# Hybrid decoder block on one core: key norms as one number per token, row spreads from rounded halves, the last expert batch in another order

## The chip, the cores and the metric

The kernel runs on one core of a Trainium2 chip. The metric is the device time of one execution in microseconds (us); the kernel before takes 690.97 us (median of 3 runs, 690.14 to 691.37). Its engines work side by side and wait for one another on semaphores: PE (TensorE, matrix products and transposes into the PSUM banks), DVE (VectorE), ACT (ScalarE), POOL (GpSimd) and SP, which issues nearly all the DMAs.

## The reference, cut to what matters

```python
u = rms_norm(h, norm1_w)                       # h: 16 meta tokens and 256 tokens, 1024 wide
proj = u @ W_in                                # differential attention q k v, delta rule q k v, gates
# branch A: differential attention, 8 heads, per-head RMSNorm of the output
# branch B: convolution over 4 tokens and SiLU on q, k, v, then
q = l2_normalize(q) * 128 ** -0.5;  k = l2_normalize(k)
gc = cumsum(g)                                 # log decays, g < 0
decay = where(incl, exp(gc[i] - gc[j]), 0)
kb = k * beta
A = where(strict, (kb @ k.T) * decay, 0);  T = inv(A + eye)
u = T @ (v * beta);  w = T @ (kb * exp(gc))
qk = (q @ k.T) * decay
k_dec = k * exp(gc[-1] - gc)
# along the chunks: v_new = u - w @ S;  o = (q * exp(gc)) @ S + qk @ v_new
#                   S = S * exp(gc[-1]) + k_dec.T @ v_new
o = rms_norm(o, norm_w) * silu(gate)
h = h + (sigmoid(gA) * (yA @ Wa) + sigmoid(gB) * (o @ Wb)) @ W_out
# mixture of experts: 32 experts of 256 hidden columns, 2 for each token
for e in range(32):
    y = y + combine[:, e:e+1] * ((silu(x @ w_gate[e]) * (x @ w_up[e])) @ w_down[e])
out = rms_norm(h + y, final_norm_w)[:, 16:]
```

## The kernel before

**Projections.** The columns of W_in, the two branch matrices and W_out are cut into 96 tiles of 128 columns; `KINDS` gives their order (ak av aq dq dk dv gate ga ya gb yd out). SP loads them in pairs into a ring of six slots. Each 32-bit tile is split into a rounded high part, `w_hi` (ACT, `split_high`, L302), and the rest, `w_lo` (DVE, `split_low`, L307), two tiles ahead; PE then takes 24 products per tile, three for each of 8 blocks (L817): high by high, high by low, low by high. Tiles alternate between two PSUM banks. So tile n waits for its two parts and for tile n-2 to be read out: by ACT (`tile_out`, counted by `tile_copied`), or by DVE alone for ya, yd and out (counted by `mixed`).

**The stage of 26 slots.** For m = 0 to 25 PE computes tile dq+m, and around it the attention heads, the convolution (DVE L1809, L1822) and the sums of squares run. The sums of squares of 8 q heads, 8 k heads and 8 attention outputs gather as 24 rows of one bank, one row by head, one column by token. After slot 20 ACT makes rows of reciprocal roots from them (`roots`, L1463 to L1467: a table load, Ln, Exp). A row must reach all 128 partitions to scale a head; `spread` (L941) does it as a 32-bit product with one column of the identity, into a bank that DVE multiplies from (`scale_by`, L1831 to L1837). In slots 22 to 25 come four spreads each: first the keys, then the queries. The eight spreads of attention follow one by one behind the first eight steps of the delta rule.

**The delta rule.** It runs for the meta tokens, chunk 0 and chunk 1 (128 tokens each) as steps s0 to s7, t1, x2, t2, x3, t3, v, o, q; for the meta tokens s0 to s7, w, m. Chunks work in two chains of four heads, a and b. `MIX_ORDER` puts half tiles of the projection between PE's steps; `BEHIND` is the matching list for ACT, DVE and POOL. In `BEHIND` a tile whose second half stood before a step is held and is read out behind that step's first chain. Step q is the norm of a chunk's output: PE sums the squares (L1110), ACT takes Ln and Exp (L1542, L1543), DVE multiplies (L2013), POOL gates (L735). Ln and Exp are in one ACT table, the tanh of the gates in another; a change costs an ACT_TABLE_LOAD.

Per-token columns hold what depends on a token and a head: `nbeta` (minus beta), `nbegc` (minus beta times exp(gc)), `kdec` (exp of the total less gc), `ngc` (minus gc, the bias in the exponent of the decay, L1501).

**Experts.** 8 batches of 4 experts (`batch`, L1200 on). PE gathers tokens (L1207), multiplies by the gate and the up matrices (L1222), turns the routing weights (L1229) and the hidden values (L1233), multiplies by the down matrices in two halves of columns (L1244), and adds the result to the tokens (L1254; L1194 in the last batch). Weights, 1 MB each, go to 12 slots and 9 twins of them; SP issues a load when its slot is free. The last batch's down matrices come in halves of columns (`load_last`, L578). Then the last norm: squares on ACT (L1651), root (L1592, L1593), scaling on DVE (L2193 to L2210), store (L623).

The wait that holds a tile's readout to its place:

```python
if what[0] == "spread": BEHIND.append(what)
else:
    BEHIND.append(what)
    BEHIND += held
    held = []
```

## Time and profile before

| | before |
|---|---|
| median of 3 runs | 690.97 us (690.14 to 691.37) |
| the profiled execution's own time | 685.91 us |
| its span, first to last instruction | 684.1 us |
| PE busy | 614.6 us (90%) |
| DVE, ACT, POOL busy | 338.8, 267.0, 42.8 us |
| moved by DMA | 156.05 MB |

The profile page has a row for each engine that gives its busy share in 40 equal slices of the span (17.1 us each) and one for the clock granted to TensorE, in tenths of full speed. Below it, the views used here are: the chain of waits (the pieces of work that follow one another to the last instruction), the timeline of one engine (each with the idle time before it and what ended it), and a table by stretches of time. Times are from the span's start.

### The profile page before, as it was taken

The numbers are of one execution on the slowest core, as the hardware profiler recorded it, in microseconds if no ns is written. First come the engines' busy times: TensorE is split into PE (matmuls) and PEld (weight loads), VectorE is DVE, ScalarE is ACT, GpSimd is POOL, SyncE is SP. The second block draws the span as 40 slices with busy tenths as digits, with TensorE's granted clock in tenths as the row PEclk, the third lists the DMA queues.
The fourth block names the chain that finished last, engine by engine and source line by source line (L and its number), as shares of the span: only waits on it lengthen the run. The fifth ranks groups of instructions, "written<-read, shape, count | busy, mean of one in ns | idle before, by whom it ended". The sixth has DMA issues, their size and how long they took to land.

```text
span 684.1 us, 14436 instructions
## 1 busy us (share of the span) xinstructions
PE 614.6 (90%) x5923; PEld 510.8 (75%) x5923; DVE 338.8 (50%) x744; ACT 267.0 (39%) x594; POOL 42.8 (6%) x92
## 2 busy tenths in 40 slices
PE   8999999999999998999899799999888856849864
PEld 7999998889988888999799799987444524425341
DVE  5443449999868658465755378624211101101102
ACT  6355458667686444235332946313101000101003
POOL 8300000000000001100310100000000000000000
PEclk9999999999999999999999999999999979788989
DMA  9945453232333331221321158899999999999992
GB/s 291 325 144 185 145 164 96 91 124 80 107 124 124 124 123 64 64 73 52 95 93 63 62 173 273 360 422 421 396 421 419 421 421 422 422 422 422 421 396 81
DMA packets 71297, 156.05 MB, mean 228 GB/s; under 512 B 7234, under 2 KB 56500, under 8 KB 59460
## 3 DMA queue, kind: packets, MB, share of 16 engines
q1 hardware_dynamic: 70048, 155.06, 60.7%
q8 instruction: 45, 0.74, 0.4%
q10 hardware_dynamic: 1188, 0.12, 0.2%
q14 instruction: 16, 0.13, 0.1%
HBM read 154.12 MB, written 1.05 MB: 227 GB/s over the span
## 4 chain that ended last, share of the span: by engine, by line
PE 61%; DVE 15%; DMA 14%; issue 4%; ACT 4%; ACTq 0%; DVEq 0%
PE bank L817 28%; DMA arena<-in_expert_w_down_dram 11%; PE bank L1244 5%; PE bank L1222 5%; PE bank L998 5%; DMA arena<-in_expert_w_gate_dram 4%; DVE w_lo L307 4%; PE bank L802 3%; DVE arena L1809 3%; PE bank L976 2%; PE bank L1207 2%; PE bank L941 2%; PE bank L1254 2%; DVE arena L1848 1%; ACT w_hi L302 1%
## 5 line engine op out<-in xcount | busy, mean ns | idle before, releaser
L817 PE MATMUL bank<-uT_hi,w_hi 128*128 128x272 f32 (+1 forms) x568 | 171.9, 303 | 5.6 <-DVE w_lo L307 3.9
L817 PE MATMUL bank<-uT_hi,w_lo 128*128 128x272 f32 (+1 forms) x568 | 162.5, 286 | 0.0
L817 PE MATMUL bank<-uT_lo,w_hi 128*128 128x272 f32 (+1 forms) x568 | 162.4, 286 | 0.0
L307 DVE TENSOR_TENSOR w_lo<-arena,w_hi 128x1024 fp32r<-128x1024 f32 x88 | 108.7, 1237 | 53.6 <-ACT w_hi L302 53.2
L817 PEld LDWEIGHTS bank<-uT_hi,w_hi 128*128 128x128 f32 x568 | 107.6, 190 | 10.2 <-issue 8.4
L817 PEld LDWEIGHTS bank<-uT_lo,w_hi 128*128 128x128 f32 x568 | 107.9, 190 | 1.4 <-issue 0.5
L817 PEld LDWEIGHTS bank<-uT_hi,w_lo 128*128 128x128 f32 x568 | 107.8, 190 | 0.0
L302 ACT ACTIVATE w_hi<-arena 128x1024 fp32r<-128x1024 f32 x88 | 92.2, 1052 | 0.5 <-DMA arena<-in_w_in_dram 0.4
L1244 PE MATMUL bank<-arena 128*32 128x512 f32 x256 | 39.8, 775 | 28.3 <-DMA arena<-in_expert_w_down_dram 25.9
L1222 PE MATMUL bank<-arena 128*32 128x256 f32 x1024 | 59.0, 390 | 5.3 <-DMA arena<-in_expert_w_gate_dram 5.3
L1222 PEld LDWEIGHTS bank<-arena 128*32 128x32 f32 x1024 | 33.5, 113 | 28.0 <-issue 7.0
L1244 PEld LDWEIGHTS bank<-arena 128*32 128x32 f32 x256 | 10.3, 137 | 51.5 <-issue 49.4
L1809 DVE SCALAR_TENSOR_TENSOR arena<-arena 128x272 f32<-128x272 f32 x72 | 37.8, 525 | 7.5 <-ACT arena L1380 5.7
L1634 ACT ACTIVATE arena<-bank 128x512 f32<-128x512 f32 x8 | 4.8, 598 | 92.0 <-PE bank L1244 92.0
L998 PE MATMUL bank<-arena 64*64 64x64 f32 x1032 | 37.7, 221 | 1.6 <-DVE arena L1948 1.6
L2156 DVE COPY arena<-bank 128x512 f32<-128x512 f32 x8 | 5.5, 691 | 67.5 <-PE bank L1244 67.5
L998 PEld LDWEIGHTS bank<-arena 64*64 64x64 f32 x1032 | 33.4, 135 | 5.9 <-DVE arena L1948 2.1
L2146 DVE COPY arena<-bank 128x256 f32<-128x256 f32 x8 | 3.4, 424 | 61.3 <-PE bank L1229 61.3
L1207 PEld LDWEIGHTS bank<-arena 128*128 128x128 f32 x256 | 29.8, 192 | 3.8 <-issue 3.8
L1207 PE MATMUL bank<-arena 128*128 128x128 f32 x256 | 30.2, 276 | 0.3 <-DVE arena L2118 0.3
L1628 ACT ACTIVATE arena<-bank,arena 128x128 f32<-128x128 f32 x32 | 9.1, 367 | 49.6 <-PE bank L1207 49.6
L1254 PE MATMUL bank<-arena 128*128 128x512 f32 x56 | 25.9, 605 | 0.0
(346 smaller groups left out, 1023.6 us busy)
## 6 DMA issues: line engine op xcount, KB each, us to landing
arena<-in_w_in_dram SPq DMA_DIRECT2D x36, 1024.0 KB, 5.2
arena<-in_expert_w_gate_dram SPq DMA_DIRECT2D x32, 1024.0 KB, 21.2
arena<-in_expert_w_up_dram SPq DMA_DIRECT2D x32, 1024.0 KB, 23.2
arena<-in_expert_w_down_dram SPq DMA_DIRECT2D x28, 1024.0 KB, 20.1
arena<-in_w_branch_attn_dram SPq DMA_DIRECT2D x4, 1024.0 KB, 5.3
arena<-in_w_branch_dn_dram SPq DMA_DIRECT2D x4, 1024.0 KB, 5.1
arena<-in_w_out_dram SPq DMA_DIRECT2D x4, 1024.0 KB, 5.4
arena<-in_expert_w_down_dram SPq DMA_DIRECT2D x8, 512.0 KB, 15.6
```

Source lines behind the costliest of these rows:

```text
L302: nc.scalar.activation(w_hi[q % NSPLIT], split_source(nc.scalar, q), ACT.Copy).then_inc(w_hi_ready, 1)
L307: nc.vector.tensor_tensor(w_lo[q % NSPLIT], src, w_hi[q % NSPLIT].bitcast(F32), ALU.subtract).then_inc(w_lo_ready, 1)
L802: last = pe.matmul(ps[:, 0:SEQ], a[:, c, t * P:(t + 1) * P], b[i][:, c, :], start=(c == 0 and k == 0), stop=(c == NC - 1 and k == 2))
L817: last = pe.matmul(ps[:, 0:b.shape[2]], a[:, c, :], b[:, c, :], start=(c == 0 and i == 0), stop=(c == NC - 1 and i == 2))
L941: pe.matmul(spread_bank(k)[:, 0:L], ident[:, SPREAD[k]:SPREAD[k] + 1].broadcast_to([P, P]), rs_rows, start=True, stop=True).then_inc(sprea ...
L976: last = pe.matmul(o[:, h, :], lhsT(h), rhs(h), start=start, stop=stop)
L998: last = pe.matmul(o[rows, h, :], lhsT[rows, h, :], rhs[rows, h, :], start=True, stop=True, tile_position=(q * Q, q * Q))
L1207: last = pe.matmul(bank[6 + group][:, (c % 4) * P:(c % 4 + 1) * P], u2[:, t, c * P:(c + 1) * P], pick[:, t].rearrange("p e s -> p (e s)"), ...
L1222: last = pe.matmul(bank[4 + 2 * m][CAP * e:CAP * (e + 1), 0:D_EXPERT], xg[:, c, CAP * e:CAP * (e + 1)], gate_up(e, odd)[:, c, m], start=(c ...
L1244: last = pe.matmul(bank[6 + half][CAP * e:CAP * (e + 1), :], hidT[:, fc, CAP * e:CAP * (e + 1)], down_of(e, odd)[:, fc, half * 512:(half + ...
L1254: last = pe.matmul(bank[2 * t + half][:, :], pickT[:, t, :], dsb[:, half * 512:(half + 1) * 512], start=False, stop=False, skip_group_chec ...
L1809: last = stt(a, x_[:, k:k + L], tap(k, c), a, ALU.mult, ALU.add)
```

## The change

- **Keys.** The keys are no longer scaled by their norms: the 8 key spreads and their 16 DVE products are gone. With r the reciprocal root of a token and head, k appears in A as r_i r_j, once on each side. PE turns the finished rows (three transposes, to bank 7), DVE copies r and the logarithm of its square's inverse out as columns (`key_columns`, slot 23), PE spreads the meta tokens' 16 rows (slot 24), and DVE folds them into the columns above (`fold_keys`, slot 25): `nbk` = nbeta times r, `nbegc` and `kdec` times r, and `ngc` minus half the logarithm, which puts r_j into the decay. `dkT_meta`, formerly written by the scaling, is now a copy on POOL.
- **Spreads.** The rows are made three times, 32 partitions apart (`one_of` has three ones). ACT rounds them to `rs_halves` and DVE takes the rest of the rows 32 to 63 as the low half; a spread is then one rounded product (`two_of` picks row i and row 32+i). 16 are left: 3, 3 and 2 of the queries' in slots 23 to 25, the attention's where they were. POOL's start has 6 more selects, 2 memsets and an add.
- **Step q.** A tile that is held is read out ahead of step q.
- **Every batch.** The routing weights are turned between gate and up, not behind up.
- **Last batch.** 16 products of the identity stand before its gate products. The first expert's down matrix comes whole; the sums onto tokens stand in another order, and the last norm is split by token tile.

```diff
@@ the delta rule's and spreads' order
-        SPREAD = [H + h for h in range(H)] + list(range(H)) + [2 * H + h for h in range(H)]
-        N_DN = 2 * H
+        SPREAD = list(range(H)) + [2 * H + h for h in range(H)]
+        N_DN = H
-            return SPREAD[4 * (m - 22):min(4 * (m - 21), N_DN)] if m >= 22 else []
+            return SPREAD[3 * (m - 23):min(3 * (m - 22), N_DN)] if m >= 23 else []
             else:
+                if what[1][2] == "q":
+                    BEHIND += held
+                    held = []
                 BEHIND.append(what)
                 BEHIND += held
@@ load_last (SP)
+                        if e == 0:
+                            if half == 0:
+                                load_unit(first_expert, True, NC)
+                            continue
@@ POOL
+            pool.wait_ge(silu_ready, 2 * H)
+            pool.tensor_copy(dkT_meta, dkT[:, :, 0:META]).then_inc(k_meta, 1)
@@ PE
-                pe.matmul(spread_bank(k)[:, 0:L], ident[:, SPREAD[k]:SPREAD[k] + 1].broadcast_to([P, P]), rs_rows,
+                pe.matmul(spread_bank(k)[:, 0:L], two_of[:, SPREAD[k]:SPREAD[k] + 1].broadcast_to([P, P]), rs_halves,
                           start=True, stop=True).then_inc(spread_ready, 1)
+                if m == 23:
+                    pe.wait_ge(rs_ready, 1)
+                    for t in range(TT):
+                        pe.transpose(bank[7][:, t * P:(t + 1) * P], rs_rows[:, TOKENS[t]], ident)
+                    pe.transpose(bank[7][0:META, 2 * P:3 * P], rs_rows[:, 0:META], ident).then_inc(k_turned, 1)
+                if m == 24:
+                    pe.wait_ge(k_own, 1)
+                    pe.matmul(bank[7][:, 3 * P:3 * P + 2 * H], spread16[0:META, :], ...).then_inc(k_spread, 1)
@@ PE, batch
+                if last_one:
+                    for _ in range(16):
+                        pe.matmul(bank[5][:, 0:P], ident, ident, start=True, stop=True)
                 pe.wait_ge(xg_a, b + 1)
...
                     last.then_inc(used, 1)
-                pe.wait_ge(picked, b + 1)
-                pe.wait_ge(ov_flag, 1)
-                for t in range(TT):
-                    last = pe.transpose(bank[5][:, t * P:(t + 1) * P], pickw[:, t].rearrange("p e s -> p (e s)"), ident)
-                last.then_inc(gathered, 1)
+                    if m == 0:
+                        pe.wait_ge(picked, b + 1)
+                        pe.wait_ge(ov_flag, 1)
+                        for t in range(TT):
+                            last = pe.transpose(bank[5][:, t * P:(t + 1) * P], pickw[:, t].rearrange("p e s -> p (e s)"), ident)
+                        last.then_inc(gathered, 1)
...
                     if last_one and half:
-                        combine_half(b, 0)
-                        pe.wait_ge(last_in, 16 * EPB)
+                        combine_part(b, 0, 0)
+                        pe.wait_ge(last_in, 16 * (EPB - 1))
...
                 if last_one:
-                    combine_half(b, 1)
+                    for half, t in ((0, 1), (1, 0), (1, 1)):
+                        combine_part(b, half, t)
@@ ACT, roots
-                link(act.activation(rs_rows[0:NSS, :], bank[7][0:NSS, 0:L], ACT.Ln, bias=c_mean_eps[0:NSS, :]))
-                act.activation(rs_rows[0:NSS, :], rs_rows[0:NSS, :], ACT.Exp, scale=-0.5, bias=c_rs[0:NSS, :]).then_inc(rs_ready, 1)
+                link(act.activation(rs_rows[0:96, :], bank[7][0:96, 0:L], ACT.Ln, bias=c_mean_eps[0:96, :]))
+                link(act.activation(rs_rows[0:64, :], rs_rows[0:64, :], ACT.Exp, scale=-0.5, bias=c_rs[0:64, :]))
+                act.activation(rs_halves, rs_rows, ACT.Copy).then_inc(rs_ready, 1)
@@ DVE, scale_by and the two new functions
-                    dst = (dqT if i < H else dkT)[:, h, :]
-                    if i >= H:
-                        tt(dkT_meta[:, h, :], dst[:, 0:META], ps[:, 0:META], ALU.mult)
-                    last = tt(dst[:, META:L], dst[:, META:L], ps[:, META:L], ALU.mult)
+                    last = tt(dqT[:, h, META:L], dqT[:, h, META:L], ps[:, META:L], ALU.mult)
+            def key_columns():
+                dve.wait_ge(k_turned, 1)
+                for a in range(2):
+                    k0 = 64 * a + H
+                    dve.tensor_copy(kc_meta[0:META, a, :], bank[7][0:META, 2 * P + k0:2 * P + k0 + H])
+                    last = dve.tensor_copy(kcols[:, a, 0:2 * H]..., bank[7][:, 0:2 * P]...[:, :, k0:k0 + H])
+                last.then_inc(k_own, 1)
+            def fold_keys():
+                dve.wait_ge(k_spread, 1)
+                for a in range(2):
+                    link(dve.tensor_tensor_reduce(tmp17[:, 0:H], bank[7][:, ...], own_head, 1.0, 0.0,
+                                                  ALU.mult, ALU.add, kcols[:, a, own]))
+                tt(nbk, nbeta, kcols[:, 0, :], ALU.mult)
+                tt(nbegc, nbegc, kcols[:, 0, :], ALU.mult)
+                tt(kdec, kdec, kcols[:, 0, :], ALU.mult)
+                link(stt(ngc, kcols[:, 1, :], -0.5, ngc, ALU.mult, ALU.add))
+                if m == 22:
+                    dve.wait_ge(rs_ready, 1)
+                    tt(rs_halves[32:64, :], rs_rows[32:64, :], rs_halves[32:64, :].bitcast(F32), ALU.subtract).then_inc(rs_halved, 1)
```

PE's order behind tile 23 of the stage (L832 and L856 turn values, L817 and L841 are the projection, L941 and L965 the spreads). Before:

```order
L832 MATMUL bank<-arena 128x128 [waits tr_copied,silu_ready]
L832 MATMUL bank<-arena 128x128
L941 MATMUL bank<-arena 128x272 [waits qk_ready] x4
L817 MATMUL bank<-uT_hi,w_hi_50 128x256 [waits tile_copied,w_lo_ready,w_hi_ready]
L817 MATMUL bank<-uT_lo,w_hi_50 128x256
```

And in the changed kernel, where L990 and L991 turn the rows:

```order
L856 MATMUL bank<-arena 128x128 [waits tr_copied,silu_ready]
L856 MATMUL bank<-arena 128x128
L965 MATMUL bank<-rs_halves,two_of 128x272 [waits o_copied,osq_ready,biased,rs_halved]
L965 MATMUL bank<-rs_halves,two_of 128x272 [waits osq_ready,o_copied,biased] x2
L990 MATMUL bank<-arena 128x128 [waits rs_ready]
L990 MATMUL bank<-arena 128x128
L991 MATMUL bank<-arena 16x128
L841 MATMUL bank<-uT_hi,w_hi_50 128x256 [waits tile_copied,w_lo_ready,w_hi_ready]
```

Four 32-bit spreads gave way to three rounded ones and three transposes.

ACT's order around step q of chunk 1 (L1536, L1537 end step o; L1387 is the readout of a gate tile; L302 the high parts). Before:

```order
L1537 ACTIVATE arena<-bank 128x512
L1540 ACT_TABLE_LOAD
L1542 ACTIVATE arena<-bank,arena 128x512 [waits dn_pe_a]
L1543 ACTIVATE arena<-arena 128x512 [waits act_step]
L1387 ACT_TABLE_LOAD [waits gate_ready]
L1387 ACTIVATE arena<-bank 128x256 [waits tile_ready]
L1542 ACT_TABLE_LOAD
L1542 ACTIVATE arena<-bank,arena 128x512 [waits dn_pe_b]
L1543 ACT_TABLE_LOAD
L1543 ACTIVATE arena<-arena 128x512 [waits act_step]
L302 ACTIVATE w_hi_50<-arena 128x1024 [waits tile_ready,slot_in2]
L302 ACTIVATE w_hi_51<-arena 128x1024 [waits tile_ready,slot_in2]
```

In the changed kernel (L1580 ends step o, L1426 is the readout, L1585 and L1586 the root, L309 the high parts):

```order
L1580 ACTIVATE arena<-bank 128x512
L1426 ACTIVATE arena<-bank 128x256 [waits gate_ready,tile_ready]
L1583 ACT_TABLE_LOAD
L1585 ACTIVATE arena<-bank,arena 128x512 [waits dn_pe_a]
L1586 ACTIVATE arena<-arena 128x512 [waits act_step]
L1585 ACTIVATE arena<-bank,arena 128x512 [waits dn_pe_b]
L1586 ACTIVATE arena<-arena 128x512 [waits act_step]
L309 ACTIVATE w_hi_50<-arena 128x1024 [waits tile_ready,slot_in2]
L309 ACTIVATE w_hi_51<-arena 128x1024 [waits tile_ready,slot_in2]
L1426 ACT_TABLE_LOAD [waits gate_ready]
L1426 ACTIVATE arena<-bank 128x256 [waits tile_ready]
L1426 ACTIVATE arena<-bank 128x256 [waits gate_ready,tile_ready]
```

Between step o and the next two high parts stood four table loads; one stands there now, and one behind them.

PE's order in the last batch, from its gate products (L1222, L1257) on. Before:

```order
L1222 MATMUL bank<-arena 32x256 [waits twin_in5,slot_in7,twin_in3,twin_in1]
L1222 MATMUL bank<-arena 32x256 x31
L1229 MATMUL bank<-arena 128x128 [waits ov_flag,picked]
L1229 MATMUL bank<-arena 128x128
L1233 MATMUL bank<-arena 128x128 [waits hid_ready]
L1233 MATMUL bank<-arena 128x128
L1244 MATMUL bank<-arena 32x512 [waits twin_in10,twin_in9,slot_in11,twin_in8,hidT_ready]
L1244 MATMUL bank<-arena 32x512 x7
L1194 MATMUL bank<-arena 128x512 [waits down_a]
L1194 MATMUL bank<-arena 128x512
L1244 MATMUL bank<-arena 32x512 [waits last_in]
L1244 MATMUL bank<-arena 32x512 x7
```

In the changed kernel, from the same place:

```order
L1266 MATMUL bank<-arena 128x128 [waits ov_flag,picked]
L1266 MATMUL bank<-arena 128x128
L1257 MATMUL bank<-arena 32x256 [waits twin_in5,slot_in7,twin_in3,twin_in1]
L1257 MATMUL bank<-arena 32x256 x31
L1270 MATMUL bank<-arena 128x128 [waits hid_ready]
L1270 MATMUL bank<-arena 128x128
L1282 MATMUL bank<-arena 32x512 [waits twin_in10,twin_in9,slot_in11,twin_in8,hidT_ready]
L1282 MATMUL bank<-arena 32x512 x7
L1228 MATMUL bank<-arena 128x512 [waits down_a]
L1282 MATMUL bank<-arena 32x512 [waits last_in]
L1282 MATMUL bank<-arena 32x512 x7
L1228 MATMUL bank<-arena 128x512 [waits down_a]
```

The turn of the routing weights moved ahead of the up products, and one of the first half's two sums moved behind the second half.

## Rows read from the trace of the kernel before

**Rows 1.** The page: the span, and the clock granted to TensorE by slice.

```profile
span 684.1 us, 14436 instructions
...
PEclk9999999999999999999999999999999979788989
```

**Rows 2.** Stretches: from:to us, length, busy (x instructions) by engine, PEclk, DMA share, GB/s.

```profile
390.00:400.00 10.00, 6.52 (x42) 6.55 (x43) 8.02 (x10) 6.86 (x11) 1.27 (x1) 0.83 0.32 105
428.00:432.00 4.00, 4.00 (x35) 3.87 (x34) 3.82 (x6) 2.88 (x4) 0.00 (x0) 1.00 0.53 158
440.00:444.00 4.00, 4.00 (x29) 3.20 (x28) 0.42 (x1) 0.91 (x4) 0.00 (x0) 1.00 1.02 426
654.00:656.00 2.00, 0.00 (x0) 0.00 (x0) 0.00 (x0) 0.00 (x0) 0.00 (x0) 0.50 1.00 416
668.00:669.00 1.00, 0.58 (x8) 0.29 (x12) 0.36 (x1) 0.00 (x0) 0.00 (x0) 1.00 0.26 90
```

**Rows 3.** Chain of waits, slots 22 to 25: start us, us, what.

```profile
205.17 1.90 PE bank L941 x8
...
212.32 2.84 PE bank L817 x24
...
222.67 0.68 PE bank L976 x4
```

**Rows 4.** Timeline, DVE, the 26-slot stage: start us, us, instruction, [idle before].

```profile
205.69 1.23 DVE L307 TENSOR_TENSOR w_lo<-arena,w_hi 128x1024 fp32r<-128x1024 f32 x1 [1.22 <-ACT w_hi L302]
214.95 1.22 DVE L307 TENSOR_TENSOR w_lo<-arena,w_hi 128x1024 fp32r<-128x1024 f32 x1
216.56 1.41 DVE L1837 TENSOR_TENSOR arena<-arena,bank 128x256 f32<-128x256 f32 x4
```

**Rows 5.** Timeline, PE, step m of the meta tokens.

```profile
246.44 0.70 PE L1095 MATMUL bank<-arena 128*128 128x512 f32 x1 [1.15 <-DVE arena L2000]
```

**Rows 6.** Timeline, PE, ACT and DVE, step q of chunk 0.

```profile
326.88 0.75 DVE L1881 TENSOR_TENSOR arena<-bank,arena 128x256 f32<-128x256 f32 x2
327.51 0.36 PE L817 MATMUL bank<-ya_hi,w_hi 128*128 128x256 f32 x1 [2.41 <-issue]
329.95 0.77 DVE L1939 TENSOR_TENSOR arena<-bank,arena 128x256 f32<-128x256 f32 x2
```

**Rows 7.** Timeline, ACT, DVE and PE, step q of chunk 1.

```profile
381.27 0.59 ACT L1537 ACTIVATE arena<-bank 128x512 f32<-128x512 f32 x1
383.89 0.63 ACT L1543 ACTIVATE arena<-arena 128x512 f32<-128x512 f32 x1
388.24 1.28 ACT L1543 ACT_TABLE_LOAD   x1
391.24 2.14 DVE L307 TENSOR_TENSOR w_lo<-arena,w_hi 128x1024 fp32r<-128x1024 f32 x1 [0.29 <-ACT w_hi L302]
393.48 0.36 PE L817 MATMUL bank<-uT_hi,w_hi 128*128 128x256 f32 x1 [3.90 <-DVE w_lo L307]
```

**Rows 8.** Chain of waits, 393 us to the end.

```profile
393.48 36.03 PE bank L817 x288
...
472.47 7.04 PE bank L1222 x128
...
656.53 9.19 PE bank L1222 x128
...
667.39 0.52 PE bank L1233 x2
...
668.41 1.97 PE bank L1244 x16
...
671.06 1.98 PE bank L1194 x4
```

**Rows 9.** Timeline, DVE, the last norm.

```profile
676.63 1.29 DVE L2193 TENSOR_TENSOR arena<-bank,arena 128x512 f32<-128x512 f32 x2 [0.98 <-issue]
...
679.63 0.74 DVE L2210 SCALAR_TENSOR_TENSOR arena<-bank,arena 128x512 f32<-128x512 f32 x1
```

77 lines of the change are left out of this document (49 added, 28 removed).

## The prediction

> **What bounds the kernel now.** I read the page first: a span of 684.1 us, PE nearly always busy, and a clock at 9 tenths or more in the first 32 slices, below it in several of the last eight [rows 1]. That hints at two halves with different limits. The table by stretches places the border. At 428 to 432 us the DMA share is still 0.53, at 440 to 444 it is 1.02 with 426 GB/s [rows 2], and by 668 to 669 it has sunk to 0.26: the expert weights have landed. In between the transfers never rest, so time saved on PE inside the expert stage is worth nothing, save behind the last landing. But the stream's start is set by slots that come free as PE finishes projection tiles. What PE gains before 430 us therefore moves the whole stream forward, and counts in full.
>
> Before 430 us the chain of waits shows PE nearly throughout. In slots 22 to 25 it runs spread groups of 1.90 us between tiles [rows 3]. I then looked for PE's idle times, since there another engine sets the pace: 1.15 us at step m [rows 5], 2.41 us at step q of chunk 0 [rows 6], 3.90 us at step q of chunk 1 [rows 7]. Behind the last one the clock is 0.83 over 390 to 400 us [rows 2], that is, partly at 1.2 GHz. The end, from 656.53 us, is a chain of PE, DVE and ACT [rows 8, 9].
>
> **The change part by part.** Sums are made against the profiled execution's own 685.91 us.
>
> *Spreads.* Four old ones take 1.90 us [rows 3], 0.47 each. A rounded product of 256 columns costs 2.84 / 24 = 0.12 us in a tile [rows 3]; a new spread has 272 columns, so 0.13. Between them a new spread could lie anywhere from 0.12 to 0.47; it is the same kind of product as the tile's, so I take 0.13. PE's own work shrinks by 8 x 0.47 for the keys and 16 x 0.34 for the rest, 9.2 us, and grows by three transposes and a small product, about 0.4. Not all of this is gained, for DVE stands right behind. Tile 23's low part starts at 205.69 and ends at 206.92 [rows 4]; PE could not start the tile before, so the four spreads at 205.17 were hidden and removing them gives nothing. ACT's extra rounding copy of the rows puts this 0.4 later. From there I go tile by tile. DVE spends in slot 22 0.36 on the low half, 1.6 on the convolution, 0.35 on SiLU, 1.2 on the split [rows 4]; tile 24 can start at about 211.45. In slot 23 it has three products of 0.35 (four took 1.41 [rows 4]) and four small copies, 0.35 together; w_lo of tile 25, which began at 214.95 [rows 4], is ready at 215.95, and that and not PE (215.15) starts tile 25. In slot 25 s0 waits for the eighth query product, at about 220.3 instead of 222.67 [rows 3]: 2.4 us gained, where PE's own work alone would have shrunk by about 6. `fold_keys`, some 0.7 us on DVE, lies behind that product and delays only w_lo of tile 27, needed 3 us later. Steps s0 to s6 then bring one shorter spread each, 7 x 0.34 = 2.4 us. The eighth brings nothing: PE already waits at step m for DVE [rows 5], and waits longer. I take 4.8 us in all. The bounds: 2.4 if DVE sets the pace in the meta steps too, 8.8 if PE sets it all along.
>
> *Costs I set near nothing.* POOL's added selects, memsets and the copy of the meta keys run in its long idle time; the constants they delay are first needed by PE behind the fourth tile. ACT's one more copy at slot 2 (`two_of`) stands in a stage where ACT and DVE set the pace: 0.1 us, at most 0.3.
>
> *Step q, chunk 0.* PE idles 2.41 us to 327.51, since the tile before must be read out, and DVE does that at 326.88 only, behind the product with the root [rows 6]. Ahead of the root these two readouts (0.75 us) can run from 324.9 on. PE gains 2.2 us there, but not for long: s2 needs DVE's L1939 at 329.95 [rows 6], which stands behind the roots' products and a split that do not move. PE would reach s2 at 329.6 instead of 331.8 and wait to 330.4. I take 1.4 us; bounds 1.0 and 2.4.
>
> *Step q, chunk 1.* ACT ends step o at 381.86 [rows 7]. The held tile is finished by PE at 382.17, so the root begins 0.55 us later than now and its first Exp ends at 385.1 to 385.3 instead of 384.52 [rows 7]. Then Ln and Exp of chain b follow at once (1.3 us), because no table load stands between: two loads of 1.28 us are gone, one of them the row at 388.24 [rows 7], one has moved behind the two high parts. These end at 388.5, the load at 389.8, the readout of the tile two before at 390.15. DVE's low part took 2.14 instead of 1.22 us beside POOL's gating [rows 7]; I leave it so, and it ends at 390.15 too. PE, free at 389.6, starts at 390.2 instead of 393.48: 3.3 us. Bounds: 1.5, and the whole 3.90. With the gap goes the clock's fall. The 12 tiles behind it took 36.03 us [rows 8], and at 2.84 each [rows 3] they would take 34.1: another 1.9 us, bounds 0 and 1.9. Together 5.2.
>
> The Trainium skill, in "ScalarE: Activation LUTs", section "What ACT_TABLE_LOAD costs", puts a switch of table at about 2.66 us, the load and a drain as long again. The rows differ: Exp starts where the load of 388.24 ends, at 389.53, with no drain to be seen. By the page two switches fewer would be worth 5.3 us, but the gap caps the gain at 3.9, so this term would be 5.8 instead of 5.2; the rows decide.
>
> *The turn of the routing weights* between gate and up saves DVE's two small steps between up and the hidden product, some 1.2 us in each batch. In seven of them PE then waits longer for DMA. In the last it counts, below.
>
> *Last batch.* Gate weights land at 656.4 whatever PE does. PE had idled since 651.7, and the clock shows 0.50 at 654 to 656 [rows 2]: 128 products took 9.19 us against 7.04 at full clock [rows 8]. The 16 new products take 16 x 0.22 = 3.6 us of the 4.85 idle; if they hold the clock, 2.15 us are gained, if they do not, none. Then up ends at 656.53 + 7.04 + 0.38 (the turns, now inside) = 663.95, and the hidden values' turn starts 0.5 later, at 664.45, instead of 667.39 [rows 8]: 2.9 us. The whole half of the down weights has landed by then: 2.5 of 4 MB, in 656.4 to 668.4, is 663.9. From the first down product (668.41 [rows 8]) to the last product of the norm (680.37 [rows 9]) it is now 11.96 us. With one sum (0.95, rows 8 have two in 1.98) instead of two ahead of the second half, the second half ends 1.0 earlier; DVE starts its norm products at +7.2 instead of +8.2 [rows 9], but the first root then waits for these two and ACT has one more square behind it, so I end at +11.1: 0.85 us. The second half's weights are there at 668.4, and PE asks at 669.1, so this wait stays hidden by 0.7 us. Together 3.8 us; bounds 0.8 and 4.6.
>
> The sum: 4.8 - 0.1 + 1.4 + 5.2 + 3.8 = 15.1 us. The profiled execution's 685.91 becomes 670.8. The runs shown have a median of 690.97, 5.06 above it; I carry that over and predict 675.9.
>
> **The rivals.**
>
> *DVE sets the pace from tile 23 on.* DVE gets low halves, key columns and folding, and tile 25 already waits for it by my sum. If PE also waits in s1 to s6, the first term is 2.4 and the readouts' gains shrink to their lower bounds: 2.4 + 1.0 + 1.5 + 1.9 + 3.8 less 0.3 is 10.3: 680.7. For it speaks w_lo at 205.69 after 1.22 idle [rows 4], against it that DVE sheds the keys' sixteen products.
>
> *The low clock stays at the end.* The products come too early or the wait outlasts them: 2.1 us less, 678.0.
>
> *The stream does not move.* If slots come free earlier but the expert weights are asked for as late as now, only the end counts: 690.97 - 3.8 = 687.2. Against it: 0.53 at 428 to 432 [rows 2] says that the queue ran dry for want of slots.
>
> *Slower: PE at half its clock through the stage it now waits in.* New idle times come before tiles 24, 25 and at steps s0 and m, with DVE in front. A single idle time of 3.9 us cost 1.9 us of clock [rows 7, 8]. At 1.2 GHz a tile takes 2.84 us more. From 212 to 246 us stand about eight tiles: if all ran low, 22.7 us would be lost against 15.1 gained: 698.6. It decides from the sixth tile on. Against it: the new idle times come to under 1.5 us each, and the slices around the 2.41 us of chunk 0 show no fall [rows 1].
>
> **How the numbers follow.** The forecast gets 0.62; its own range is 672.5 to 680. DVE's pace 0.13, the low clock at the end 0.08, the stream that does not move 0.10, slower 0.05; 0.02 is left for no difference. The range runs from 671, where the first term is 4 us above my value (its own bound) and a step q at its cap, to 684, between the first rival and the third; about 0.18 lies outside. A change within 0.2% (1.4 us) cannot be told from none. Three rivals are faster, one is slower: faster 0.92, same 0.02, slower 0.06.
>
> **What would show it.** Right: s0 of the meta tokens at about 220.3; no idle time of PE over 0.7 us at 325 us and at 385 us, shifted by the gains before; step m's wait grown to 1.5 us; the DMA share at 1.0 from 425 us or so instead of 435; the last gate landing near 645.1; its 128 products in 7.1 us; from the first down product to the last norm product 11.1 us. Wrong: tile 25 later than 216.9, which would mean that DVE is worse than counted; a gap before the steps s2 to s6; an unchanged start of the full DMA share; or a PE clock of 0.5 anywhere before 430 us.

## The result and the profile after

The changed kernel takes **675.26 us** (median of 4 runs, 674.86 to 675.57) against 690.56 us for the kernel before beside it: ratio 0.9779, interval 0.9766 to 0.9792. I had predicted 675.9. A second measurement on another occasion gave 675.54 against 688.76, ratio 0.9823 (0.9795 to 0.9851). So the gain is 13 to 15 us. The point hit more exactly than its terms deserve: the terms that I had named were too large by 3.4 us in sum, most of it in the spreads, and a gain that I had not named and the offset that I carried over made up for it. All this is told below.

The page of the changed kernel; each digit of PEclk and DMA is one of 40 slices:

```profile
span 673.6 us, 14458 instructions
PE 610.8 (91%) x5928; PEld 509.7 (76%) x5928; DVE 337.0 (50%) x738; ACT 265.2 (39%) x594; POOL 47.4 (7%) x102
PEclk9899999999998999999999999999998969788899
DMA  9864552324333523222231358899999999999993
```

PE's busy time has shrunk by 3.8 us only (614.6 before), the span by 10.5. That does not make the gain mostly idle time: the busy time now holds the 16 added products (3.74 us) and what two stretches of low clock cost, told next. PEclk has an 8 in the second slice that the kernel before did not have [rows 1], and that is the first thing to clear away. Some of PE's rows behind 29 us, of the changed kernel (start, duration, engine, line, operation, shapes, count), show products of 272 columns that follow each other by 0.23 us, up to 33.67, where they then take their usual 0.13:

```profile
29.14 0.43 PE L841 MATMUL bank<-uT_lo,w_hi 128*128 128x272 f32 x1
29.37 0.43 PE L841 MATMUL bank<-uT_hi,w_lo 128*128 128x272 f32 x1
...
33.87 0.29 PE L841 MATMUL bank<-uT_lo,w_hi 128*128 128x272 f32 x1
33.99 0.28 PE L841 MATMUL bank<-uT_hi,w_lo 128*128 128x272 f32 x1
```

PE was never idle there, and the clock stood at 1.2 GHz, half of full (PEclk 0.50), all the same. It costs time before anything that the change touches: the tile of slot 21 starts at 203.64 instead of 200.72, 2.92 us late. In the fourteen profiles of this study that delay is 0 four times (the kernel before twice, two variants of the changed one), 1.4 to 1.7 us five times and 2.4 to 3.0 us five times, one of these a variant of the kernel before (the experiment with the halves alone). Two profiles of one kernel agree in it each time (0 and 0 us before, 2.92 and 2.90 changed); it is the variants that differ, with the same instructions up to that tile in most of them. I therefore count **from the tile of slot 21**, and call its start T: 200.72 before, 203.64 after, 203.62 in the second profile of the changed kernel.

The places that the prediction spoke of, as PE's timeline of the changed kernel has them (where a row ends at the border of the stretch that was asked for, its time and its count are those of a part, here and below):

```profile
208.17 0.41 PE L856 MATMUL bank<-arena 128*128 128x128 f32 x2 [1.27 <-ACT arena L1441]
210.43 0.36 PE L841 MATMUL bank<-uT_hi,w_hi 128*128 128x272 f32 x1 [1.85 <-issue]
212.11 0.43 PE L841 MATMUL bank<-uT_lo,w_hi 128*128 128x272 f32 x1
220.51 0.35 PE L841 MATMUL bank<-uT_hi,w_hi 128*128 128x256 f32 x1 [0.66 <-issue]
224.92 0.71 PE L1011 MATMUL bank<-arena 128*128 128x128 f32 x4 [0.90 <-ACT arena L1441]
246.97 1.55 PE L1130 MATMUL bank<-arena 128*128 128x512 f32 x3 [1.50 <-DVE arena L2068]
325.90 0.35 PE L841 MATMUL bank<-ya_hi,w_hi 128*128 128x256 f32 x1 [0.37 <-issue]
330.87 0.68 PE L1033 MATMUL bank<-arena 64*64 64x64 f32 x16 [0.53 <-DVE arena L2007]
389.17 0.36 PE L841 MATMUL bank<-uT_hi,w_hi 128*128 128x256 f32 x1 [0.69 <-ACT arena L1426]
```

The idle time of 2.41 us at step q of chunk 0 [rows 6] has become 0.37, that of 3.90 in chunk 1 [rows 7] 0.69, and that of 1.15 at step m [rows 5] has grown to 1.50. The two rows at the top are new: 1.27 and 1.85 us ahead of tile 23. The table by stretches of the same kernel (us; PE busy, PEld, DVE, ACT, POOL; PEclk, DMA share, GB/s) has what they did to the clock, and the stream's start:

```profile
210.00:212.00 2.00, 1.57 (x10) 1.60 (x11) 1.87 (x5) 1.52 (x4) 0.00 (x0) 0.83 0.20 29
212.00:214.00 2.00, 2.00 (x11) 2.00 (x10) 1.89 (x3) 0.00 (x0) 0.00 (x0) 0.50 0.98 336
388.00:400.00 12.00, 11.31 (x96) 11.14 (x95) 9.89 (x14) 8.22 (x13) 1.17 (x1) 1.00 0.54 176
424.00:428.00 4.00, 4.00 (x35) 3.92 (x34) 3.82 (x6) 1.73 (x3) 0.00 (x0) 1.00 0.82 279
428.00:432.00 4.00, 4.00 (x36) 4.00 (x36) 3.08 (x4) 0.89 (x4) 0.00 (x0) 1.00 1.01 426
```

The clock of 388 to 400 us is 1.00 (0.83 over 390 to 400 before) and the DMA share of 428 to 432 is 1.01 (0.53 before) [rows 2]. And the end, PE's timeline again:

```profile
649.02 1.29 PE L1257 MATMUL bank<-arena 128*32 128x256 f32 x20 [1.45 <-DMA arena<-in_expert_w_gate_dram]
652.61 0.44 PE L1266 MATMUL bank<-arena 128*128 128x128 f32 x2
657.25 0.51 PE L1270 MATMUL bank<-arena 128*128 128x128 f32 x2 [0.61 <-DVE arena L2220]
658.27 1.92 PE L1282 MATMUL bank<-arena 128*32 128x512 f32 x16 [0.52 <-DVE arena L2222]
660.91 1.12 PE L1228 MATMUL bank<-arena 128*128 128x512 f32 x2 [0.72 <-ACT arena L1677]
662.76 1.49 PE L1282 MATMUL bank<-arena 128*32 128x512 f32 x12 [0.72 <-DMA arena<-in_expert_w_down_dram]
```

All together, from T on, in us; the last column has the gains with the second profile of the changed kernel (the end of the span goes by the page's value, which is rounded to 0.1):

| stretch | before | after | gain | second |
|---|---|---|---|---|
| T to step m's product | 45.72 | 43.33 | 2.39 | 2.35 |
| to s2 of chunk 0, behind step q | 85.36 | 83.90 | 1.46 | 1.50 |
| to the tile behind step q, chunk 1 | 61.68 | 58.30 | 3.38 | 3.36 |
| the 12 tiles behind it | 36.03 | 34.53 | 1.50 | 1.52 |
| to the last gate landing | 227.02 | 225.32 | 1.70 | 0.88 |
| to the first down product | 11.88 | 9.25 | 2.63 | 2.63 |
| to the end of the span | 15.69 | 15.33 | 0.36 | 1.16 |
| sum | 483.38 | 469.96 | **13.42** | **13.40** |

The second profile of the kernel before differs from the first in three of these stretches: 36.70 us for the 12 tiles, 227.3 to the last gate landing, 11.50 to the first down product. Against it the sum of the gains is 14.0 us.

### The profile page after: what moved, and what is told of

The parts are those of the page before. It is cut to its first block, busy times and chain, and to the rows that moved or that the text cites. A ratio compares the mean times of both kernels' runs of the same rounds, so it can differ in the third digit from the quotient of the medians.

```text
span 673.6 us, 14458 instructions
## 1 busy us (share of the span) xinstructions
PE 610.8 (91%) x5928; PEld 509.7 (76%) x5928; DVE 337.0 (50%) x738; ACT 265.2 (39%) x594; POOL 47.4 (7%) x102
## 4 chain that ended last, share of the span: by engine, by line
PE 62%; DMA 15%; DVE 9%; ACT 7%; SPq 3%; issue 3%; ACTq 0%; DVEq 0%
PE bank L841 31%; DMA arena<-in_expert_w_down_dram 15%; PE bank L1033 5%; PE bank L1282 5%; PE bank L826 3%; PE bank L1257 3%; SPq L594 3%; DVE w_lo L314 2%; PE bank L1011 2%; ACT w_hi L309 2%; PE bank L1238 2%; PE bank L942 2%; PE bank L1293 1%; PE bank L910 1%; DVE arena L1854 1%
## 5 line engine op out<-in xcount | busy, mean ns | idle before, releaser
L841 PE MATMUL bank<-uT_hi,w_hi 128*128 128x272 f32 (+1 forms) x568 | 171.3, 302 | 4.9 <-issue 3.8
L841 PE MATMUL bank<-uT_hi,w_lo 128*128 128x272 f32 (+1 forms) x568 | 163.5, 288 | 0.0
L841 PE MATMUL bank<-uT_lo,w_hi 128*128 128x272 f32 (+1 forms) x568 | 163.2, 287 | 0.0
L841 PEld LDWEIGHTS bank<-uT_hi,w_hi 128*128 128x128 f32 x568 | 108.8, 192 | 9.0 <-issue 7.4
L841 PEld LDWEIGHTS bank<-uT_lo,w_hi 128*128 128x128 f32 x568 | 108.9, 192 | 1.1 <-issue 0.5
L841 PEld LDWEIGHTS bank<-uT_hi,w_lo 128*128 128x128 f32 x568 | 108.6, 191 | 0.0
L309 ACT ACTIVATE w_hi<-arena 128x1024 fp32r<-128x1024 f32 x88 | 92.2, 1052 | 0.7 <-DMA arena<-in_w_in_dram 0.5
L1282 PE MATMUL bank<-arena 128*32 128x512 f32 x256 | 38.0, 745 | 32.8 <-DMA arena<-in_expert_w_down_dram 31.2
L1257 PE MATMUL bank<-arena 128*32 128x256 f32 x1024 | 58.6, 380 | 1.5 <-DMA arena<-in_expert_w_gate_dram 1.4
L1282 PEld LDWEIGHTS bank<-arena 128*32 128x32 f32 x256 | 9.8, 133 | 55.2 <-issue 51.5
L1257 PEld LDWEIGHTS bank<-arena 128*32 128x32 f32 x1024 | 32.5, 110 | 22.5 <-issue 3.1
L2211 DVE TENSOR_TENSOR arena<-bank,arena 128x512 f32<-128x512 f32 x8 | 5.5, 692 | 39.8 <-PE bank L1238 39.8
```

Of the source, the lines that this page charges most:

```text
L309: nc.scalar.activation(w_hi[q % NSPLIT], split_source(nc.scalar, q), ACT.Copy).then_inc(w_hi_ready, 1)
L841: last = pe.matmul(ps[:, 0:b.shape[2]], a[:, c, :], b[:, c, :], start=(c == 0 and i == 0), stop=(c == NC - 1 and i == 2))
L1257: last = pe.matmul(bank[4 + 2 * m][CAP * e:CAP * (e + 1), 0:D_EXPERT], xg[:, c, CAP * e:CAP * (e + 1)], gate_up(e, odd)[:, c, m], start=(c ...
L1282: last = pe.matmul(bank[6 + half][CAP * e:CAP * (e + 1), :], hidT[:, fc, CAP * e:CAP * (e + 1)], down_of(e, odd)[:, fc, half * 512:(half + ...
```

## The experiments

Each ran in three or five rounds beside the kernel before. As the early delay moves a total by up to 3 us, whatever the kernel, I read each also from its T.

**1. The kernel before, again.**

> The kernel before, unchanged, for a second profile. Theory A: the profiled execution of 685.91 us was an unusual one; another has a low clock in the first 40 us like the changed kernel's (27 to 34 us, 0.50, tile 3 in 5.5 us instead of 3.3), and its own time is about 690. Theory B: the low clock at 27 us comes from the change (POOL's longer start); then this profile has the clock at 1.00 there and its time is near 686.

Measured: 689.69 us, ratio 1.0007 (0.9985 to 1.0030). Its profile (span 684.7) has no low clock at 27 us and the landmarks of the first to 0.01 us up to 393.48. So the numbers of theory B came here, not those of A. But B's cause, POOL's longer start, does not by itself bring the delay: two variants of the changed kernel have that start and a delay of 0.06 and 0.07 us (experiments 5 and 6). That the delay comes by chance, in the kernel before too, is not shown by any profile; the one variant of the kernel before that has it (2.80 us) has the longer start as well. It is only made likely by the runs. Among the eleven later runs of the kernel before, the profiler gives a mean clock of 0.963 for three, which took 685.7 to 686.7, and 0.958 for five, which took 688.5 to 690.8: there too runs are about 3 us apart. A mean lower by 0.005 over 685 us would be some 7 us more at half clock, an estimate that fits the 6.8 us of the changed kernel's profile, but where those us lie in these runs is not recorded.

**2. The narrow products of the start moved apart.**

```diff
-                if n == 2:
-                    ba_logit_products()
+                if 2 <= n <= 4:
+                    ba_logit_products((n - 2,))
```

> The changed kernel with the 72 narrow products of 16 columns (for beta and the decay logits) behind tiles 2, 3 and 4, 24 each, instead of all behind tile 2. Theory A: the low clock from 27 to 34 us comes from 4 us of narrow products in one piece; apart, the clock stays at full, and about 2.8 us are gained: 672.5. Theory B: the clock falls there for another reason: 675.3.

Measured: 674.11 us, ratio 0.9783 (0.9742 to 0.9823). In its profile the low clock lies at 8 to 11 us, not behind 25 us, and T is 1.36 late. Inconclusive: the delay took another place, and a single profile can't say whether the edit or chance moved it.

**3 and 4. Idle products where the first four spreads had been.** First on both sides of the turn in slot 22, later behind it alone:

```diff
+                if m == 22:
+                    pe.wait_ge(biased, ATT_UNITS)
+                    keep_clock(bank[2], 5)
                 if m >= 18 and m - 2 < 24:
                     ...
                     tr_values(h, ("dv", h), acc[:, (m - 2) % NACC, :], False)
+                if m == 22:
+                    keep_clock(bank[2], 7)
```

> The changed kernel with 5 + 7 products of the identity (0.22 us each) around the turn of values in slot 22, where PE idles 1.26 and 1.85 us. Theory A: the idle time dropped the clock, and tile 23 took 4.8 instead of 3.05 us; kept busy, tile 23 takes 3.05 to 3.2 us and the kernel gains 1.7 us over the changed one: about 673.6. Theory B: the clock falls for another reason, or DVE's chain sets s0 anyway: no gain, 675.3.

> Six idle products behind the values' turn of slot 22 alone, which end before the tile can start. Clock theory (the 1.6 us that tile 23 takes too long is the low clock after the idle time of 1.85): the tile starts where it started, 2.3 us behind the turn's start, takes 3.25 us instead of 4.7, and all that follows comes 1.4 us earlier: s0's product 17.0 us behind the turn instead of 16.7 plus 1.4 less, so 15.2 to 15.4; total 1.4 less than the changed kernel's. Rival (s0 waits for the roots' halves on ScalarE and VectorE anyway, not for the tiles): tile 23 is short, but the wait ahead of s0 grows from 0.9 to 2.3 us and the total does not move.

The second had the wait and six products behind the turn, none ahead of it. Measured: 673.12 us, ratio 0.9773 (0.9729 to 0.9816); and 674.26 us, ratio 0.9801 (0.9771 to 0.9832), beside 675.54 for the changed kernel in the same rounds. PE's timeline of the second one, and its table by stretches:

```profile
202.30 0.36 PE L841 MATMUL bank<-uT_hi,w_hi 128*128 128x272 f32 x1 [0.42 <-issue]
207.08 1.17 PE L779 MATMUL bank<-arena 128*128 128x128 f32 x9
209.09 0.36 PE L841 MATMUL bank<-uT_hi,w_hi 128*128 128x272 f32 x1 [0.51 <-issue]
222.09 0.71 PE L1014 MATMUL bank<-arena 128*128 128x128 f32 x4 [0.91 <-ACT arena L1444]
```

```profile
209.00:212.00 3.00, 2.91 (x23) 2.94 (x24) 2.88 (x6) 1.19 (x2) 0.00 (x0) 1.00 0.55 158
212.00:216.00 4.00, 4.00 (x36) 3.98 (x35) 3.29 (x8) 2.67 (x7) 0.00 (x0) 1.00 0.42 148
```

From T to s0's product it is 19.79 us in both; in the changed kernel 21.28, in the kernel before 21.95. The tile starts where it did (6.79 behind T) and takes 3.26 instead of 4.77. So 1.5 us of the missing gain was the clock, and the rival, that s0 would wait longer, is refuted: its wait is 0.91 as before. The gap ahead of the turn, 1.27, does no harm alone. This is the better kernel up to the end of the 12 tiles, which comes 218.5 us behind T in both and 220.1 in the changed kernel. Behind them it is not seen to last: with the second kernel the last gate landing comes 228.1 us later, where the changed kernel has 225.3 and 226.1, and from T to the end it takes 470.4 us, against 470.0; the first has 225.4 and ends 468.4 behind T. In total the second one's 1.28 us are within the scatter of both (671.62 to 676.74, and 674.12 to 678.34), so it is not shown that the total is faster.

**5. Tiles read out behind the roots, as before.**

```diff
-                if what[1][2] == "q":
-                    BEHIND += held
-                    held = []
```

> The changed kernel, held tiles read out behind step q's first chain again. Theory: chunk 0's part gives back 1.4 us, chunk 1's 3.3 us and the low clock behind it 1.5 us: 6.2 us, 681.5. Rival: the clock alone does not follow the gap: 4.7 us, 680.0. Rival: the expert stream sets the end and none of it is seen: 675.3.

Measured: 682.98 us, ratio 0.9908 (0.9870 to 0.9946), 9.9 us over the kernel of experiment 3, which ran beside it and has the cover as well. Both gaps are back, and the low clock with the second, by PE's timeline and the table by stretches:

```profile
325.03 0.36 PE L837 MATMUL bank<-ya_hi,w_hi 128*128 128x256 f32 x1 [2.45 <-issue]
390.90 0.36 PE L837 MATMUL bank<-uT_hi,w_hi 128*128 128x256 f32 x1 [3.94 <-DVE w_lo L314]
```

```profile
390.00:400.00 10.00, 9.10 (x64) 9.13 (x65) 7.75 (x12) 5.61 (x9) 0.00 (x0) 0.83 0.38 118
```

From its T of 200.79 the span ends after 476.01 us, in the changed kernel after 469.96 and 469.98: 6.0 us, against 6.6 in my sum (1.4 + 5.2). The medians say more, 9.9 less the 1.5 of the cover, so some 8 us; but the profiled execution was one of the two fastest of six (678.48; the slowest took 685.24), its T had no delay, and what the slower ones lost is not seen. The tile of 390.90 comes 4.6 later than in the changed kernel, and the 12 tiles take 36.03 instead of 34.5. No other part of the change measured so is worth as much.

**6 and 7. The same delay ahead of the stream, and within it.**

```diff
+                if n == FIRST["yd"]:
+                    keep_clock(bank[7], 18)
```

and, as the other kernel, `keep_clock(bank[5], 18)` behind the second batch.

> Adds 18 idle products of 128 x 128 (about 4 us in the rows of such products) ahead of the first tile of the output projection, from which on the experts' weights are read. Theory: the weights' stream starts when TensorE frees its buffers and has no slack of its own, so all later landmarks and the last landing move by the added time: total +4.0 us over the changed kernel. Rival: the stream starts by DMA or other work and is bound by its own bytes, so the last landing stays and the total grows by 0 to 1 us.

> Adds the same 18 products behind the second batch of experts, while the weights stream. Theory: TensorE has slack against the stream there, so the waits for weights shrink by the added time and the total grows by 0 to 0.5 us. Rival: TensorE is the bound among the experts too, and the total grows by 4.0 us as in the run before.

Measured, in the rounds in which the changed kernel took 675.54: **679.42** us ahead of it (ratio 0.9877, 0.9850 to 0.9903) and **675.60** within it (0.9812, 0.9788 to 0.9835). The products, which stand ahead of the first `yd` tile in the one kernel, took 4.0 us in either. Ahead of the stream they count in full, 3.9 us by the medians and 4.7 from T. Within it the medians show nothing, as PE waits less for DMA: the wait of 2.16 us for the down weights at 517.80 of the changed kernel's profile in these rounds is gone, and the next has shrunk from 8.72 to 7.66 us, here in the timeline of the kernel with the delay within the stream:

```profile
546.89 1.93 PE L1282 MATMUL bank<-arena 128*32 128x512 f32 x8 [7.66 <-DMA arena<-in_expert_w_down_dram]
```

The last gate landing comes 446.1 us behind T, in the changed kernel 445.4 and 446.2. Only behind it this profile loses time, 1.7 us to a low clock (experiment 8), so that from T it is 1.6 us longer in all; the medians do not have it. That the stream starts when PE lets it, and then takes what it takes, is the prediction's premise, shown from both sides. The changed kernel itself ran a second time here:

> The changed kernel unchanged, run again beside the three below. Chance theory: the low clock at 27 to 34 us of its first profile is luck, so this profile has it at another place or not at all, and all landmarks from slot 18 on stand up to 2.9 us earlier (first product of step m's tile at about 244, down product of the last batch at about 655.4), own time 672.5 to 675.4. Change theory: the spell belongs to the changed kernel's front; it is there again at 27 us with the landmarks of the first profile, own time 675.4. In both theories tile 23 of the front takes 4.7 us at a low clock after the waits of 1.3 and 1.9 us, since those are in the instruction order.

Its profile has the low clock at 27 to 34 us again, so the number asked for by the chance theory did not come; what speaks for chance is the variants without it and the spread of the runs, not this run. The last gate landing is 0.8 us later behind T, and the end differs from the first profile's in one place, the wait of 0.72 for the last load, which the second does not have, as PE's timeline shows:

```profile
649.82 2.53 PE L1257 MATMUL bank<-arena 128*32 128x256 f32 x41 [2.09 <-DMA arena<-in_expert_w_gate_dram]
659.07 1.50 PE L1282 MATMUL bank<-arena 128*32 128x512 f32 x12 [0.52 <-DVE arena L2222]
662.77 1.49 PE L1282 MATMUL bank<-arena 128*32 128x512 f32 x12
```

**8. Without the 16 products of the last batch.**

```diff
-                if last_one:
-                    for _ in range(16):
-                        pe.matmul(bank[5][:, 0:P], ident, ident, start=True, stop=True)
```

> The changed kernel without the 16 idle products ahead of the last gate product. Theory (they keep the clock up over the last gate, up and down products): the two groups of 64 products and the turn between them take 9 us or more at half clock instead of 8.2, and with the combining products after them the kernel ends 1.2 to 2.1 us later. Rival (the clock stays up by itself, since TensorE is less idle now): no change, within 0.3 us from the last landing to the end.

Measured: 676.62 us, ratio 0.9808 (0.9773 to 0.9843). From the landing to the first down product 12.07 us instead of 9.25, more than either theory allowed, and 0.19 more than in the kernel before. PE's timeline, and the stretch in which the weights land:

```profile
647.74 2.79 PE L1253 MATMUL bank<-arena 128*32 128x256 f32 x24 [3.45 <-DMA arena<-in_expert_w_gate_dram]
654.15 0.44 PE L1262 MATMUL bank<-arena 128*128 128x128 f32 x2
659.81 0.64 PE L1278 MATMUL bank<-arena 128*32 128x512 f32 x4 [0.52 <-DVE arena L2218]
```

```profile
647.00:651.00 4.00, 3.26 (x32) 1.79 (x36) 0.00 (x0) 0.00 (x0) 0.00 (x0) 0.50 1.01 419
```

The gate products take 6.48 instead of 3.65 us, as the 3.45 us of idle time let the clock fall to 1.2 GHz. The total is 1.1 to 1.4 us over the changed kernel's two medians, within the scatter (673.97 to 678.63); from T it is 2.0. In experiment 7 the landing came late as well: the 16 products stood there, PE was then idle for 3.56 us, and the gate products took 5.35. So the products held the clock where the weights landed at most 2.1 us behind them, and not at 3.56 us.

**9. The last batch's order as before.** `load_last` loads by halves again, `combine_half` and the norm over both tiles stand again as in the old lines of the diff.

> The changed kernel with the last batch's load, combining products and norm in the order of the kernel before; the 16 products and the turn of the routing weights stay. Theory: the stretch from the first down product to the end is 0.4 us longer (it was 15.69 us before and 15.33 after), 0.85 if my step was sized rightly; total +0.4 to +0.85. Rival: the new order only moved a wait for the last load, which the changed kernel has at 0.72 us, and the stretch does not change: total within 0.2 us.

Measured: 675.71 us, ratio 0.9800 (0.9761 to 0.9840). From the first down product (657.17) to the end it is 15.63 us. Of the ten profiles with the new order seven have 14.5, the second one of the changed kernel among them, one has 14.7, and two have 15.3, one of them the first: in these two PE waits 0.7 us for the last load. The kernel before has 15.69. So the new order is mostly worth 1.1 us, and 0.4 when the last load comes late, always by the profiles: the total does not show it (672.45 to 679.29). The rows of PE's timeline in the old order:

```profile
657.17 1.07 PE L1280 MATMUL bank<-arena 128*32 128x512 f32 x8 [0.52 <-DVE arena L2217]
664.47 1.98 PE L1224 MATMUL bank<-arena 128*128 128x512 f32 x4 [0.81 <-DVE arena L2219]
```

The second wait of PE for DVE's hidden values, 0.81 ahead of the last sums, exists only in this order.

**10. The routing weights turned behind up.** The block with `if m == 0:` stands behind the loop over gate and up again.

> The changed kernel with the turn of the routing weights back behind the up products, in every batch. Theory: it costs the length of the turn in the last batch alone, where nothing hides it: +0.44 us by its row, less what the wait for the hidden values hides, so +0.2 to +0.6 us from the last landing to the first down product; the four batches before wait for weights anyway. Rival: it counts in all five batches, 5 times 0.4 = 2.0 us.

Measured: 674.78 us, ratio 0.9778 (0.9747 to 0.9809), no difference in the total. The idle time ahead of the hidden values' turn is 1.30 us again, twice that of the changed kernel, and from the gate products' start to the first down product it is 9.80 instead of 9.25: 0.55 us, once. The rival's 2.0 us are refuted: from T to the end it is 469.8 us, as in the changed kernel. PE's row:

```profile
658.02 0.51 PE L1268 MATMUL bank<-arena 128*128 128x128 f32 x2 [1.30 <-DVE arena L2218]
```

**11. Rounded halves in the kernel before, keys still scaled.** The new `rs_halves`, `two_of` and their rounding in the kernel before; all 24 spreads stay, from slot 22 on.

```diff
-                pe.matmul(..., ident[:, SPREAD[k]:SPREAD[k] + 1].broadcast_to([P, P]), rs_rows,
+                pe.matmul(..., two_of[:, SPREAD[k]:SPREAD[k] + 1].broadcast_to([P, P]), rs_halves,
```

> The kernel before with the spreads as rounded halves alone: all 24 are kept, four in a slot, and the keys are still scaled by them; nothing else of the change. Theory (VectorE sets the pace once the spreads are short): four spreads fall from 1.90 to 0.5 us a slot, but four scalings of 1.22 us and the rest of a slot's VectorE work do not fit a tile and its turns, so the first product of step m's tile comes at most 1.5 us earlier than in the kernel before, relative to the same tile of slot 20, and the total gains 0 to 1.5 us. Rival (the spreads' time on TensorE is all that counts): five slots by 1.4 us, 5 to 7 us less.

Measured: 688.82 us, ratio 0.9999 (0.9975 to 1.0023): nothing. Four spreads are now 0.81 us instead of 1.90, and the time goes into waits and a low clock, as in PE's timeline of this kernel:

```profile
210.71 0.81 PE L952 MATMUL bank<-rs_halves,two_of 128*128 128x272 f32 x4 [2.26 <-DVE rs_halves L1914]
211.54 0.43 PE L828 MATMUL bank<-uT_lo,w_hi 128*128 128x272 f32 x1
226.68 0.68 PE L987 MATMUL bank<-arena 128*128 128x128 f32 x4 [1.18 <-ACT arena L1413]
248.13 1.98 PE L1106 MATMUL bank<-arena 128*128 128x512 f32 x4 [1.47 <-DVE arena L2018]
```

From T (203.52) to s0 23.16 us, against 21.95 before: 1.2 later. To step m 44.61 against 45.72: 1.1 earlier, since the meta steps gave 2.3. The cheap spread alone buys nothing in front, as the first theory forecast, and in the end even its 1.1 us can't be told from none. But that VectorE's pace is the cause is not shown: tile 23 ran at the low clock here too, 4.69 us instead of 3.26, and without these 1.4 us s0 would come up to 0.2 us earlier than before. With the keys' norms as numbers per token, which take sixteen products from DVE and eight spreads from PE, s0 comes at 21.28, under the same low clock: 1.9 us earlier than here. Which of the two gave it was not separated.

## Why the prediction was right, and where it was not

*The premise.* PE sets the stream's start, the stream takes what it takes, and the end is a chain. Experiments 6 and 7 show it. "The stream does not move" is refuted. From the last tiles' end to the last landing, though, the stream does not take quite the same: 227.0 to 227.5 us in the three profiles of the kernel before and its variant, 225.3 to 226.3 in nine of the changed kernel and its variants, but 227.2 and 228.1 in two more (experiments 6 and 4). Neither the 16 products, nor the last batch's order, nor the turn of the routing weights makes the difference: without each of them it is 225.3, 225.6 and 225.4. It stays open, and with it 0.9 to 1.7 us of the gain.

*Spreads: 4.8 predicted, 2.4 measured. The step that failed is "the four spreads at 205.17 were hidden and removing them gives nothing".* It was true of the tile's start: it comes 2.26 us behind the turn of the values in both kernels (the turn itself is 0.5 us later, the 0.4 that I had given ACT's copy). But the hidden spreads had kept PE busy through the wait. Without them it stood still for 1.85 us and ran tile 23 at half clock, which cost 1.5 us. This is the mechanism of my slower rival in small; I had set it aside because "the new idle times come to under 1.5 us each", and one of them came to 1.85. My own sign for being wrong, a PE clock of 0.5 before 430 us, is in the trace. With the cover of experiment 4, s0 comes 2.16 us earlier, where I had said 2.4. The remaining 0.7 are in the meta steps, which gave 1.7 where I had 2.4. The price of 0.34 per spread was right: in experiment 11, with the same short spreads, the meta steps gave 2.3. What I had not counted is that PE, now earlier, waits there for DVE. From s1 to s3 it takes 4.01 us in experiment 11 and 4.51 in the changed kernel (PE's timelines, the changed kernel first), and the later steps take the same in both:

```profile
228.60 0.33 PE L1058 MATMUL bank<-arena 64*64 64x64 f32 x4
233.11 0.45 PE L1033 MATMUL bank<-arena 64*64 64x64 f32 x8 [0.31 <-DVE arena L2016]
```

```profile
230.27 0.33 PE L1034 MATMUL bank<-arena 64*64 64x64 f32 x4
234.28 0.45 PE L1009 MATMUL bank<-arena 64*64 64x64 f32 x8
```

So the rival "DVE sets the pace from tile 23 on" holds for 0.5 us between s1 and s3 (s1 itself comes 0.1 later behind s0 than in experiment 11), and the gap before s3 is another of my signs for being wrong. Step m's wait grew to the 1.5 us that I had worked out.

*`two_of` and POOL's start.* No cost of theirs can be seen; the two profiles with T unshifted stand 0.06 and 0.07 behind the kernel before's 200.72, where I had said 0.1; the delay at 27 us, whose cause is open, is left out of this.

*Step q: chunk 0 1.4 predicted, 1.5 measured; chunk 1 3.3 and 1.9 predicted, 3.4 and 1.5 measured*, and 6.0 of 6.6 by experiment 5. The chain of readouts, roots and table loads came as worked out. The clock's part was 0.4 too high against the first profile because I let the 12 tiles run at 2.84 us each; they run at 2.88 (34.53 / 12). Against the second profile of the kernel before, whose low clock lasted longer, it is 2.2, 0.3 more than I had said. The gap's part, 3.4, bears on the price of a table load, for which I let the row decide (1.28 us, Exp right behind it) over the 2.66 us that the Trainium skill gives in "ScalarE: Activation LUTs", section "What ACT_TABLE_LOAD costs": by the page it would have been the whole 3.9. The load that is left shows no drain either, in ACT's timeline of the changed kernel, where the readout starts 0.01 us behind it:

```profile
387.35 1.28 ACT L1426 ACT_TABLE_LOAD   x1
388.64 0.66 ACT L1426 ACTIVATE arena<-bank 128x256 f32<-128x256 f32 x2
```

*Last batch: 3.8 predicted, 3.0 and 3.8 measured.* The warm clock and the early turn gave 2.6 of 2.9; of these the products alone are worth 2.8 (experiment 8) and the turn 0.55 (experiment 10), together more than 2.6: the 128 products took 9.19 us in the kernel before [rows 8] and 6.48 + 3.66 = 10.1 in experiment 8, where the clock came back later. Why later, after a shorter idle time, stays open; that moment varies between profiles of one kernel too, as the second one of the kernel before has 8.80 us for the 128 products and 11.50 to the first down product. The chain behind it gave 1.16 of 0.85 in the second profile, 0.36 in the first, where the wait for the last load that I had called "hidden by 0.7 us" showed with 0.72.

*The sum and the offset.* Against the 15.1 us of my terms stand 11.7 in the stretches that they name, or 12.5 with the second profile. The 1.7 or 0.9 up to the last landing, in no term of mine, bring the sum to the 13.4 measured from T. That the time came out at 675.3 is due to the offset of 5.06 us from the profiled execution to the median: the profiled execution of before had no delay at its start and the changed kernel's had one of 2.9, which its median of 675.26 contains too, as far as its four runs, all within 0.6 us of the profiled one, can tell. The offset between a profile and a median was thus not the constant that I took it for (it is -0.1 for the changed kernel), and the predicted own time, 670.8 us, was missed by 4.6 (675.37), or by 1.7 without the delay. The hit is luck to that extent. The gain of 13.2 in the second measurement agrees with the sum from T; that of 15.3 in the first is 1.9 more, for which no profile has the reason.

## What to carry to other kernels

- Before removing work that is hidden behind another engine's wait, ask what the engine's clock does without it. Here a gap of 1.85 us left in that way cost 1.5 us, and six idle products in it gave them back at the next landmarks. They ended 0.5 us before the awaited tile could start; in the last batch, idle products that ended 3.56 us too early let the clock fall.
- A tile's readout that is queued behind a chain of roots holds up the engine that fills the tile: issuing two short copies ahead of the chain was worth 6 us here from T, nearly half of the change, at no cost in work.
- Profiles of near variants can differ by 3 us at a place that no edit between them touches. Count from a landmark behind it, and do not carry an offset between profile and median over from a single profile.

## What the hardware showed that I had not expected

- TensorE's clock fell to 1.2 GHz behind idle times of 1.27 and 1.85 us close together (PEclk 0.83, 0.50), but stayed at 2.4 GHz where the second was filled, with the first still there (1.27 and 0.51). All ten profiles that leave the second unfilled have the fall. Behind 3.90 us it cost 1.5 us in the tiles that follow, or 2.2 in the second profile, behind 1.85 it cost 1.5.
- It fell at 27 to 34 us with PE busy throughout, for 6.8 us in the first profile of the changed kernel, and for 3.4 or 6.8 in eight of fourteen profiles; each time during or right behind the products of 16 columns that PE runs there from 24 us on. Three profiles run low somewhere between 7 and 12 us, instead or as well. Five that have the 16-column products in one piece have no fall behind them, so these products alone don't set it off; what does wasn't found.
- VectorE's subtraction that took 2.14 us beside GpSimd's gating [rows 7] also took 2.29 us in the changed kernel, from 387.96 on, where it was 1.23 at 209.10; and GpSimd's product beside it took 2.19 us, where its first took 1.30.
